# The recurrence's inverses in 32-column form for four of their levels

## The reference, cut to what matters

```python
def step(state, inp):
    r_t, w_t, k_t, v_t, a_t, b_t = inp
    sa = jnp.einsum('bhvk,bhk->bhv', state, a_t)
    state = (state * w_t[:, :, None, :]
             + sa[..., None] * b_t[:, :, None, :]
             + v_t[..., None] * k_t[:, :, None, :])
    y_t = jnp.einsum('bhvk,bhk->bhv', state, r_t)
    return state, y_t
```

## Time and profile before

| | before |
|---|---|
| median of three runs | 1403.82 us |
| profiled execution, its own time | 1402.62 us |
| span of its trace | 1400.4 us |
| mean granted TensorE clock | 0.95 |
| PE busy | 1255.3 us, 90% |
| DVE busy | 940.1 us, 67% |
| ACT busy | 630.4 us, 45% |
| POOL busy | 208.5 us, 15% |

### The profile page before, as it was taken

One profiled execution on the slowest core, in us unless ns is written; L12 is line 12 of the kernel. 1 busy time (PEld: TensorE's weight loads), 2 busy tenths in 40 slices (PEclk: granted clock), 3 DMA queues, 4 the chain that ended last, 5 costly groups with the idle time before them and its releaser, 6 DMA issues.

```text
span 1400.4 us, 21886 instructions
## 1 busy us (share of the span) xinstructions
PE 1255.3 (90%) x9218; PEld 1167.3 (83%) x9218; DVE 940.1 (67%) x1298; ACT 630.4 (45%) x829; POOL 208.5 (15%) x139
## 2 busy tenths in 40 slices
PE   3998989887899999699888889999789887999995
PEld 3887878775899999696667888999789877999995
DVE  6767657544468874755864567774548835999994
ACT  4464343224443445456556564434442244544442
POOL 0000000000264442000000122210000001344431
PEclk9999999898999999899998999999899997999998
DMA  7440001000577764253322668785342213545530
GB/s 269 151 154 31 32 1 61 1 1 1 196 268 246 247 214 154 90 184 117 119 92 95 216 246 286 268 288 181 121 151 91 90 61 120 175 164 185 186 135 30
DMA packets 122656, 200.20 MB, mean 143 GB/s; under 512 B 3264, under 2 KB 111168, under 8 KB 112320
## 3 DMA queue, kind: packets, MB, share of 16 engines
q1 hardware_dynamic: 117664, 168.05, 35.7%
q0 software_dynamic: 3456, 25.17, 4.8%
q10 hardware_dynamic: 1440, 5.60, 1.1%
HBM read 197.75 MB, written 1.05 MB: 142 GB/s over the span
## 4 chain that ended last, share of the span: by engine, by line
PE 63%; DVE 24%; ACT 7%; issue 5%; DMA 0%; DVEq 0%; POOL 0%; ACTq 0%
PE bank L631 13%; PE bank L632 12%; PE bank L633 12%; DVE buf L2390 7%; DVE ring_r L1696 6%; PE bank L714 3%; PE bank L716 3%; PE bank L715 3%; ACT high L1173 2%; DVE work L1952 2%; PE bank L647 2%; PE bank L869 2%; DVE work L1948 2%; PE bank L857 2%; PE bank L1065 1%
## 5 line engine op out<-in xcount | busy, mean ns | idle before, releaser
L631 PE MATMUL bank<-part,high 128*128 128x256 f32 x1664 | 485.8, 292 | 66.6 <-DVE part L1703 61.5
L632 PE MATMUL bank<-part,high 128*128 128x256 f32 x1664 | 481.7, 289 | 0.0
L1696 DVE TENSOR_TENSOR ring_r<-ring,high 128x2048 fp32r<-128x2048 f32 (+1 forms) x155 | 342.9, 2221 | 206.3 <-ACT high L1173 204.0
L633 PE MATMUL bank<-part,ring_r 128*128 128x256 f32 x1664 | 481.1, 289 | 0.0
L631 PEld LDWEIGHTS bank<-part,high 128*128 128x128 f32 x1664 | 329.4, 198 | 75.3 <-issue 52.6
L632 PEld LDWEIGHTS bank<-part,high 128*128 128x128 f32 x1664 | 329.5, 198 | 0.3 <-issue 0.2
L633 PEld LDWEIGHTS bank<-part,ring_r 128*128 128x128 f32 x1664 | 329.1, 198 | 0.0
L1173 ACT ACTIVATE high<-ring 128x2048 fp32r<-128x2048 f32 x155 | 295.2, 1906 | 51.1 <-PE bank L633 40.9
L1623 POOL TENSOR_TENSOR ring_r<-ring,high 128x512 fp32r<-128x512 f32 x44 | 95.4, 2167 | 534.0 <-ACT high L1173 533.9
L714 PE MATMUL bank<-part,high 128*128 128x256 f32 x528 | 151.3, 287 | 9.2 <-POOL part L1617 4.9
L715 PE MATMUL bank<-part,high 128*128 128x256 f32 x528 | 150.1, 284 | 0.0
(11 more groups left out here) (260 smaller groups left out, 1580.9 us busy)
## 6 DMA issues: line engine op xcount, KB each, us to landing
ring<-in_wide SPq DMA_DIRECT2D x122, 1024.0 KB, 5.9
ring<-in_down SPq DMA_DIRECT2D x33, 1024.0 KB, 5.0
buf<-in_wide POOLq DMA_DIRECT2D x24, 1024.0 KB, 7.2
con<-in_cons SPq DMA_DIRECT2D x1, 1472.0 KB, 10.9
ring<-in_wide SPq DMA_DIRECT2D x2, 576.0 KB, 7.0
buf<-in_wide ACTq DMA_DIRECT2D x1, 1024.0 KB, 5.4
buf<-in_wide SPq DMA_DIRECT2D x1, 1024.0 KB, 5.3
buf<-in_ctx_t ACTq DMA_DIRECT2D x1, 1024.0 KB, 4.7
```

Source lines behind the costliest of these rows:

```text
L631: mm(bank, ah, bh, start=start, stop=False, skip_group_check=shared)
L632: mm(bank, ah, bl, start=False, stop=False, skip_group_check=shared)
L633: return mm(bank, al, bh, start=False, stop=stop, skip_group_check=shared)
L1696: v.tensor_tensor(low, raw, hi.bitcast(F32), ALU.subtract).then_inc(sem("unit_low"), 1)
```

## The change

`x` (the inverse so far) is kept as the 32 columns of its own square: for row i of a matrix only the 32 columns of i's square are stored, so that the four matrices take 128 columns and not 512. The wide form that remains is the transpose `xt`. Up to level 4:

- y is now `near`^T x and dx is xt^T y, with 32 moving columns for each matrix (128 for each group) where there were 128 (512); weights stay 128 by 128. ACT evicts 128 columns, and the join covers 128.
- y needs only the join; dx needs `xt`. DVE makes the transpose in four instructions, one for each of the four row squares (32 partitions, four matrices), since source and destination columns differ.
- Level 0 works on `xt` (a join of 512 columns), then forms `near`, the scores inside the squares (a product of 512 columns), then transposes back into `x` in four instructions.

Level 5 uses `far` (two copies on ACT for each group, after level 1) for y; its dx is two matmuls for each matrix, with weights of 64 and of 96 columns. Two small DVE transposes for each group out of PSUM put the result into `xt`; PE's transposes and their evictions go. ACT assembles the left half of x for level 6 (two copies and one eviction for each group). Scores are made transposed, with one more 64 by 64 by 64 matmul for each of the eight banks. Two zero fills for each of two tiles are put at the start on DVE, and 384 columns of masks (192 KB) are added to the load.

```diff
@@ scores, PE
-                                mm(bank[:, 0:P], at_, bt_, start=True, stop=True)
+                                mm(bank[:, 0:P], bt_, at_, start=True, stop=True)
+                                mm(bank[CH:P, 0:CH], at_[:, CH:P], bt_[:, 0:CH], start=True, stop=True)
@@ levels, PE
-                            xt = work[:, g % 2, 2, :]
+                            near, far, xt, _, x = chain_parts(g)
                             if l <= SQUARE:
-                                pe.wait_ge(sem(f"xt_ready{g % 2}"), SQUARE * (g // 2) + l)
+                                pe.wait_ge(sem(f"x_ready{g % 2}"), SQUARE * (g // 2) + l)
                             else:
-                                wait_freed(pe, ("xt", g, l - 1))
+                                wait_freed(pe, ("dx", g, SQUARE))
+                            if l == SQUARE:
+                                pe.wait_ge(sem(f"far_ready{g % 2}"), g // 2 + 1)
...
-                                    last = mm(bank[:, s_], scores[g % 2][:, j, 0:P], xt[:, s_], start=True, stop=True)
+                                    last = mm(bank[:, j * SQ:(j + 1) * SQ], (near if l < SQUARE else far)[:, s_], x[:, j * SQ:(j + 1) * SQ], start=True, stop=True)
...
+                            if l <= SQUARE:
+                                pe.wait_ge(sem(f"xt_ready{g % 2}"), SQUARE * (g // 2) + l)
+                            else:
+                                pe.wait_ge(sem(f"x_left{g % 2}"), g // 2 + 1)
                             for j in range(4):
-                                s_ = slice(j * P, (j + 1) * P)
-                                if what == "dx":
-                                    last = mm(bank[:, s_], y[:, s_], x[:, s_], start=True, stop=True)
+                                y_ = y[:, j * SQ:(j + 1) * SQ]
+                                if l < SQUARE:
+                                    last = mm(bank[:, j * SQ:(j + 1) * SQ], xt[:, j * P:(j + 1) * P], y_, start=True, stop=True)
+                                elif what == "dx":
+                                    mm(bank[0:CH, (4 + j) * SQ:(5 + j) * SQ], xt[:, j * P:j * P + CH], y_, start=True, stop=True)
+                                    last = mm(bank[0:P - SQ, j * SQ:(j + 1) * SQ], xt[:, j * P + SQ:(j + 1) * P], y_, start=True, stop=True)
...
-                        if SQUARE <= l < LEV - 1:
-                            for g in pair:
-                                x = work[:, g % 2, 1, :]
-                                wait_freed(pe, ("dx", g, l))
-                                bank = open_bank(("xt", g, l))
-                                for j in range(4):
-                                    s_ = slice(j * P, (j + 1) * P)
-                                    last = nc.tensor.transpose(bank[:, s_], x[:, s_], ident)
-                                close(last, ("xt", g, l))
@@ ACT
+                def far_blocks(g):
...
+                    own.go(act_(far[0:SQ, :, SQ:CH], scores[g % 2][0:SQ, :, SQ:CH], ACT.Copy))
+                    act_(far[CH:CH + SQ, :, CH + SQ:P], scores[g % 2][CH:CH + SQ, :, CH + SQ:P], ACT.Copy).then_inc(sem(f"far_ready{g % 2}"), 1)
...
+                            if l < LEV - 1:
+                                release(act_(chain_parts(g)[3], bank_of(key)[:, 0:P], ACT.Copy), key)
...
+                        if l == SQUARE:
+                            for g in pair:
+                                left_diagonal(g)
+                            own.settle()
+                            for g in pair:
+                                left_corner(g)
@@ DVE, start
+                for i in range(2):
+                    own.go(v.memset(work[:, i, 1, :], 0.0))
+                    own.go(v.memset(work[0:CH, i, 3, 2 * P:4 * P], 0.0))
                 v.memset(eps_norm, NORM_EPS).then_inc(sem("eps_ready"), 1)
@@ DVE, levels
-                        v.transpose(work[:, g % 2, 2, :], work[:, g % 2, 1, :]).then_inc(sem(f"xt_ready{g % 2}"), 1)
+                        xt, x = squares(chain_parts(g)[2]), squares(chain_parts(g)[4])
+                        for b in range(4):
+                            r = slice(b * SQ, (b + 1) * SQ)
+                            dst, src = (xt[r, :, r], x[r, :, :])[::-1 if back else 1]
+                            ins = v.transpose(dst, src)
+                            own.go(ins) if b < 3 else ins.then_inc(sem(f"{'x' if back else 'xt'}_ready{g % 2}"), 1)
...
-                        own.step(joined(g, 0, scores[g % 2][:, :, 0:P]))
-                        turned(g)
+                        eng.sem_inc(sem("scores_in"), 1)
+                        v.copy_predicated(squares(xt), spread(const("left_right"), [P, 4, P]).bitcast(I32), scores[g % 2][:, :, 0:P])\
+                            .then_inc(sem(f"xt_ready{g % 2}"), 1)
+                        own.go(v.tensor_tensor(squares(near), scores[g % 2][:, :, 0:P], spread(const("near"), [P, 4, P]), ALU.mult))
+                        eng.wait_ge(sem(f"xt_ready{g % 2}"), SQUARE * (g // 2) + 1)
+                        own.settle()
+                        turned(g, True)
...
-                                release(joined(g, l, bank_of(key)[:, :].rearrange("p (j n) -> p j n", j=4)), key)
-                                if l < SQUARE:
-                                    wait_freed(eng, key)
-                                    turned(g)
+                                x = squares(chain_parts(g)[4])
+                                block = bank_of(key)[:, 0:P].rearrange("p (j n) -> p j n", j=4)
+                                v.copy_predicated(x, spread(const("joins", (l - 1) * SQ, SQ), [P, 4, SQ]).bitcast(I32), block).then_inc(sem(f"x_ready{g % 2}"), 1)
+                                eng.wait_ge(sem(f"x_ready{g % 2}"), SQUARE * (g // 2) + l + 1)
+                                eng.sem_inc(free[jobs[key][0]], 1)
+                                turned(g, False)
+                            elif l == SQUARE:
...
+                                own.go(v.transpose(xt[0:SQ, :, SQ:CH], block[0:SQ]))
+                                release(v.transpose(xt[CH:CH + SQ, :, CH + SQ:P], block[CH:CH + SQ]), key)
```

More of the change, by code:

```diff
@@ L23 @@
 SQUARE = 5
+SQ = 32
 NG = KT
@@ L71 @@
         ("conv_b", FT), ("conv_w", 9 * FT), ("b_ada", 48)]
-CONS = [("ident", P), ("ones", P), ("head_sum", P), ("right_left", LEV * P), ("left_right", LEV * P), ("score_mask", 4 * P), ("rope_swap", P), ("cos", S), ("sin", S)]
+CONS = [("ident", P), ("ones", P), ("head_sum", P), ("right_left", LEV * P), ("left_right", LEV * P), ("score_mask", 4 * P), ("later", P), ("near", P), ("joins", (SQUARE - 1) * SQ), ("rope_swap", P), ("cos", S), ("sin", S)]
 ROWS = [("sgu_g", 512), ("sgu_b", 512), ("b_spatial", 512), ("lam", 256), ("c", 2 * D)]
@@ L287, in build @@
             for l in range(1, LEV):
-                for what in ("y", "dx") if l < SQUARE else ("y", "dx", "xt") if l < LEV - 1 else ("y", "dxt"):
+                for what in ("y", "dx") if l < LEV - 1 else ("y", "dxt"):
                     for g in pair:
@@ L490, in build, with chain_parts, left_of, wide_y @@
         y_sq = buf[11]
+        def chain_parts(g):
+            t = work[:, g % 2]
+            return t[:, 0, :], t[:, 1, :], t[:, 2, :], t[:, 3, 0:P], t[:, 3, P:2 * P]
+        def left_of(g):
+            return work[0:CH, g % 2, 3, 2 * P:4 * P].rearrange("p (j n) -> p j n", j=4)
+        def wide_y(g):
+            return work[0:CH, g % 2, 3, 0:4 * CH]
+        def squares(t):
+            return t.rearrange("p (j n) -> p j n", j=4)
         mix_of = [2, 1, 4, 5, 0, 3]
@@ L861, in _ @@
                         for g in pair:
-                            _, x, xt, y = (work[:, g % 2, i, :] for i in range(4))
+                            _, _, xt, y, _ = chain_parts(g)
                             wait_freed(pe, ("y", g, l))
@@ L1027, in context_states @@
                         for d in range(2):
-                            tri = const("score_mask", (0, 2)[d] * P)
+                            tri = const(("later", "score_mask")[d], (0, 2)[d] * P)
                             for t in range(TT):
@@ L2412, in constants @@
     z["left_right"] = np.concatenate([m.T for m in lv], 1)
-    z["score_mask"] = np.concatenate([i > j, i <= j, i < j, i <= j], 1)
+    z["score_mask"] = np.concatenate([(i < j) | ((i >= CH) & (j < CH)), i <= j, i < j, i <= j], 1)
+    z["later"] = i > j
+    z["near"] = (i < j) & (i // SQ == j // SQ)
+    z["joins"] = np.concatenate([np.take_along_axis(m, i // SQ * SQ + np.arange(SQ)[None, :], 1) for m in lv[1:SQUARE]], 1)
     z["head_sum"] = i // CH == j // CH
```

41 lines of the change are left out of this document (27 added, 14 removed).

## The result

The changed kernel takes 1480.84 us (median of four runs, 1479.46 to 1483.37); the kernel before took 1403.9 beside it. The ratio is 1.054, with an interval of 1.051 to 1.057: 77 us slower. The forecast was 1440, and its range ended at 1458. The direction came out as forecast, and so did the place of the larger part, the stretch from first y to sa0; the size did not, above all in the scores. The profiled execution has a span of 1477.7 us for 1400.4, at a mean granted clock of 0.891 for 0.95. One of the ten executions of experiment 8's kernel (1429.28 us) is counted as slow and stands outside its ratio.

The account below looks back on a forecast made before the run. No engine was full; PE and DVE took turns in the levels. Pairs 1, 2, 0 and 3 added 6.3 + 6.3 + 7.9 + 16.3 = +36.8 us to 1402.62, so 1439.4 (1440.6 by the median), taken as 1440; range 1410 to 1458.

Parts of the forecast that it names:

- The mechanism of the levels: Levels 1 to 4: clock halves during level 2 in pairs 0 to 2, pair 3 never recovers; 6.8 us a level, PE-bound.
- The price of a narrow product: Levels 1 to 4: eight records with 32 columns cost 1.0 us at full clock, 1.7 at half.
- the second rival: In the levels the clock falls but narrow products are cheaper, a level 4.6 us: about 1405 us, chance 0.04.
- The third rival: In the levels the clock comes and goes, or falls only at level 4: +18, 1421 us, chance 0.12.
- The scores: Score banks: two added records cost 0.16 us a bank, 1.3 us in pairs 0 to 2, 0.9 in pair 3.
- Level 5 to sa0: Stretch from level 5 to sa0 in a pair: 13.2 us together at half clock.
- Two dx 4.3 (16 records each with smaller weights): Level 5's second products, two groups: 4.3 us at half clock.
- The levels around the fall: Pair 1's levels 1 to 4: 3.4 at full clock, 5.2 falling, 7.3 with the Ln, then 6.8 us.
- After pair 3: Behind pair 3's sa0: +2.9 us up to the state at half clock, and 1.5 for what follows.
- The first rival: The clock stays at 1.00 in the levels: -11.9, so 1391 us, faster; chance 0.10.
- What was costed at nothing: Ahead of the levels: zero fills hidden in DVE's first wait, extra masks loaded before the scores need them; no added time.

Follow-up runs that it names:

- experiment 8: Changed kernel without the added score product, levels 1 to 4, 5 and 6 reading wider moving operands, against the kernel before: 1408.78 us, ratio 1.003.
- experiment 2: Changed kernel with levels 1 to 4 reading their 32 moving columns four times over (128 columns): 1447.16 us, ratio 1.033 to the kernel before.
- experiment 1: Kernel before with only the 64 by 64 by 64 score product added to each of a pair's eight banks: 1426.68 us, ratio 1.016.
- experiment 5: Kernel before with a fifth score product of the full form in each bank, the first one issued twice: 1414.8 us, ratio 1.009.
- experiment 9: Kernel before with the 64 by 64 score products added behind both heads' four products of a chunk: 1413.19 us, ratio 1.007.
- experiment 10: Kernel before with one more score product a bank, 64 moving columns on unchanged 64 by 128 weights: 1411.03 us, ratio 1.003.
- experiment 11: Kernel before with level 6's 64 moving columns read twice, rerun in more rounds: 1395.13 us, ratio 0.994.

## Why the prediction was wrong, and where it was right

**The mechanism of the levels: right.** Forecast: the clock falls in level 2 of pairs 0 to 2, pair 3 never recovers, a level is then 6.8 us and PE-bound. The trace has the fall around the start of level 3 in pairs 0 and 1, already in level 1 in pair 2, and levels of 6.83 us with no idle PE. The price of a narrow product (1.7 at half clock, from rows of 64 columns) holds, and the second rival is out: eight records took 1.91 to 1.92 us. At full clock I took 1.0 a product; it is 0.85 (two in 1.70, 116.35 to 118.05). Experiment 2 shows the clock to be the cause of the slow levels 1 to 4 rather than a companion, and the narrow products to be what brought it down. The clock came from the row with PE busy 2.00 of 2.00 at 0.50. The Trainium skill, "TensorE: Matmul & The Clock Gate", Part 1, lets the clock fall after idleness and rise when PE is busy; read as plain busyness it is contradicted again here, by 20.00 busy us of 20 at 0.50 in the kernel after. In experiment 2 a less busy PE (15.59 of 20) kept 1.00. The third rival, a clock that comes and goes or falls only at level 4, was not seen: in no pair of the changed kernel did it return before sa0.

**The scores: the step that failed most.** "Two more take between nothing and 0.2; I take 0.16" a bank gave 4.8 us; measured 23.3. I priced the added product by its records alone. The rows had no product of another shape between products of 64 by 128, so 0.2 was no upper bound: part of the overlap of the two heads was itself at stake, and a bank took 1.11 us for 0.56. In pair 2, where the clock then falls, 5.7 us more came on top. Experiments 1, 5, 9 and 10 show that neither one more product (0.22 a bank) nor one of 64 columns (0.22) does this, and that half as many changes of shape cost 2.64 us a pair for 4.38. How much of it is the change of shape, from 0.11 to 0.22 us each, and how much the small product itself, they don't separate; nor was a 64 by 64 product run whose result goes to the first 64 rows of the bank instead of the last. The Trainium skill, "TensorEngine Tiling (Array Packing)", Tiling Modes, says under its key properties that a change of the tiling mode drains TensorE. The traces agree: kept shape, 0.77 us a bank; changed shape, 1.11.

**Level 5 to sa0: too small.** Forecast 13.2 us at half clock, measured 15.84 in pair 1 (207.58 to 223.42). The terms for y (3.4, measured 3.53), for level 6 (3.8, 4.04) and for q0 (1.7, 1.76) hold. "Two dx 4.3 (16 records each with smaller weights)" fails: it is 6.51, 0.20 us a record, nearly the 0.21 of full weights of 128 by 128. I had given weights of 64 and 96 columns a discount that the pair of them doesn't have. That is some 2.2 of the 2.6 us missing in each of four pairs.

**The levels around the fall: somewhat too small.** First y to level 5's y took 24.2, 23.5 and 26.2 us in pairs 0 to 2 for a forecast 22.7. Level 1 at full clock was not 3.4; pair 0 has 4.43 and 4.36 for levels 1 and 2 (y at 116.35, 120.78 and 125.14), with the key sum inside the first, and level 3 took 8.6 and 8.2 in pairs 0 and 1, where I had 7.3. In pair 2 the clock fell in level 1, which makes level 2 6.69 us for pair 1's 3.77; its scores had been at half clock, but the projection of r behind them had brought the clock back. Pair 3 was 28.4 for 28.0. From scores to first y the 2.0 us for a forecast 1.6 is luck: pair 0 gained 0.6 and pair 2 lost 1.7, where I had +0.6 and 0.

**After pair 3: too small.** "+2.9 and 1.5 for what follows." Timeline of PE in the kernel after, sa0, the state and the first product beyond the recurrence:

```profile
375.87 1.91 PE L934 MATMUL bank<-work 128*128 128x64 f32 x8
...
382.12 0.80 PE L937 MATMUL bank<-work,buf 128*128 128x128 f32 x2
...
399.50 0.67 PE L718 MATMUL bank<-buf,con 128*128 128x512 f32 x1 [0.67 <-ACT buf L1422]
```

sa0 to the state is 6.25 us for 3.40, the 2.9 forecast. But from the state to L718 it is 17.38 us, where the kernel before took 10.25 (312.81 to 323.06): the clock stayed at 0.50 through the gate products, the second chunk and the outputs. That is 7.1 in place of 1.5.

**The first rival would have been wrong too.** It gave 1391 if the clock stayed. Experiment 8 keeps it in most of the levels, drops the score product as well, and still does not beat the kernel before. In levels 1 to 4 DVE is in the way. A transpose was taken at 0.25 us and takes 0.33 from start to start (four in 1.30); the join came out at 0.30 for 0.35. In pairs 0 to 2 DVE's work with its preparation is then 5.05 us a level, where I had 4.3 at the busiest, and 6.76 with the Ln chain, where I had 5.4. In pair 3 it is 4.24 for 3.8. One transpose of 128 by 512 in 0.71 was cheaper than the four that replaced it. So DVE eats what the levels should have gained, and they end at 83.1 us for 82.7 (80.3 in experiment 2). The loss lies behind them: level 5 to sa0 takes 12.2 us in pairs 0 to 2 of experiment 8 and 11.6 in pair 3, where I had 9.5 and 8.0 at full clock. Of that, 0.8 us in pair 0 is the doubling of level 6's columns (experiment 11), which the change doesn't have. The rest I put down to level 5's dx (4.56 us), the term that failed at half clock too; that is read from the trace and wasn't tested by a run.

**What was costed at nothing** stayed there: the zero fills lie before DVE's first wait, which is now 4.34 us, and the scores start at 99.40 us for 99.31, so the masks were in time. The narrow levels put into the kernel before, with nothing else of the change, were not run.

## What to carry to other kernels

Before narrowing a product, look in the trace for what the narrower form buys at the same weights: here 64 columns cost what 128 did, and 32 hardly less (sixteen records in 1.70 us for 1.86 at full clock, none less at half clock), while the granted clock fell to half and stayed there beyond the stretch. Where a matmul of another tile shape is put between matmuls that overlap in different rows of the array, price the loss of overlap and not the records alone, and keep the shape if you can. And look for stretches at half clock behind a run of narrow products: reading the same columns twice can be faster than reading them once.

## What the runs showed of the hardware beyond that

- A 64 by 64 product among 64 by 128 products costs 0.55 us at full clock; a 64 by 128 product, with 64 or with 128 moving columns, costs 0.22 in the same banks.
- Doubling level 6's moving columns made the untouched kernel 0.4 to 0.6% faster, by 9 us in the last runs: the clock stayed at 1.00 where it had been at 0.50.
- At half clock and with 32 moving columns a float32 record took 0.18 us on weights of 64 columns, 0.23 on 96 and 0.21 on 128 (211.11, 211.46 and 211.92: 0.81 us for two records of 64 and two of 96).
- DVE's transposes of 32 by 128 take 303 ns each and start 0.33 us apart, nearly half of the 0.71 us that a transpose of 128 by 512, sixteen times the elements, takes in one instruction.
